# Six modulation units' column products moved from before the first expert pair to behind the last scatter, rank products placed directly behind the routing mask

## The reference

```python
mod = jax.nn.silu(c) @ w_ada[layer] + b_ada[layer]          # 6 x 1024 values
sh1, sc1, g1, sh2, sc2, g2 = jnp.split(mod[:, None, :], 6, axis=-1)
...
hcur = rms_norm(x, norm2_g[layer]) * (1 + sc2) + sh2
x = x + g2 * hierarchical_moe(hcur, ...)                    # top-1 group of 4, top-2 experts in it
```

## Time and profile before

| what | us |
|---|---|
| three runs: median, lowest, highest | 1336.81, 1328.77, 1337.17 |
| profiled execution | 1328.29 |
| its span | 1326.6 |
| TensorE busy (share of the span) | 1217.2 (92%) |
| VectorE, ScalarE, GpSimd busy | 358.3, 291.9, 79.5 |

### The profile page before, as it was taken

One profiled execution on the slowest core, in us unless ns is written; L12 is line 12 of the kernel. 1 busy time (PEld: TensorE's weight loads), 2 busy tenths in 40 slices (PEclk: granted clock), 3 DMA queues, 4 the chain that ended last, 5 costly groups with the idle time before them and its releaser, 6 DMA issues.

```text
span 1326.6 us, 17378 instructions
## 1 busy us (share of the span) xinstructions
PE 1217.2 (92%) x7164; PEld 716.8 (54%) x7167; DVE 358.3 (27%) x1005; ACT 291.9 (22%) x584; POOL 79.5 (6%) x135
## 2 busy tenths in 40 slices
PE   4799999999999969977989999996799999999996
PEld 1566544634344348554354444342686877767772
DVE  0202514312111124851341122211140342342212
ACT  2212423100100121134211111001201455452101
POOL 2000011000000004000000000000000233200000
PEclk8899999899999989977979999999899999999998
DMA  9994999899999995520579999999434344334000
GB/s 337 316 382 168 309 334 368 349 426 428 429 428 428 421 330 159 176 78 0 223 301 401 425 430 428 429 427 396 165 127 149 121 147 147 113 106 139 0 16 32
DMA packets 89682, 351.18 MB, mean 265 GB/s; under 512 B 5108, under 2 KB 7324, under 8 KB 77340
## 3 DMA queue, kind: packets, MB, share of 16 engines
q1 hardware_dynamic: 83144, 340.94, 66.4%
q0 software_dynamic: 4960, 6.53, 2.3%
q10 hardware_dynamic: 1524, 2.95, 0.6%
HBM read 349.27 MB, written 1.13 MB: 264 GB/s over the span
## 4 chain that ended last, share of the span: by engine, by line
PE 79%; DMA 10%; ACT 4%; DVE 3%; issue 1%; SPq 1%; DVEq 0%; ACTq 0%
PE bank L423 26%; PE bank L703 20%; PE bank L435 12%; DMA ring<-in_moe_w_up 8%; PE bank L675 3%; PE bank L724 3%; DMA ring<-in_ev_w_in 2%; PE bank L458 2%; PE bank L471 2%; PE bank L933 1%; ACT arena L1001 1%; SPq L340 1%; PE bank L554 1%; PE bank L591 1%; PE bank L480 1%
## 5 line engine op out<-in xcount | busy, mean ns | idle before, releaser
L423 PE MATMUL bank<-arena,ring 128*128 128x256 f32 x1600 | 352.7, 382 | 7.4 <-DVE arena L1385 2.8
L703 PE MATMUL bank<-ring,arena 128*32 128x512 f32 x3072 | 336.3, 595 | 8.9 <-issue 4.5
L423 PEld LDWEIGHTS bank<-arena,ring 128*128 128x128 f32 x1600 | 303.3, 191 | 55.5 <-issue 8.3
L703 PEld LDWEIGHTS bank<-ring,arena 128*32 128x32 f32 x3072 | 101.6, 110 | 230.9 <-issue 228.2
L435 PE MATMUL bank<-ring,arena 128*128 128x512 f32 x352 | 157.7, 608 | 2.4 <-issue 2.4
L435 PEld LDWEIGHTS bank<-ring,arena 128*128 128x128 f32 x352 | 68.0, 195 | 88.9 <-issue 88.0
L458 PE MATMUL bank<-ring,c_rep 128*32 128x512 f32 x480 | 62.6, 655 | 12.5 <-DMA ring<-in_w_ada 8.3
L675 PEld LDWEIGHTS bank<-arena 128*128 128x128 f32 x512 | 62.6, 203 | 11.7 <-issue 11.7
L675 PE MATMUL bank<-arena 128*128 128x128 f32 x512 | 65.5, 290 | 0.0
L1753 DVE TENSOR_TENSOR arena<-arena,bank 128x512 f32<-128x512 f32 x16 | 11.0, 687 | 198.0 <-PE bank L703 198.0
L1048 ACT ACTIVATE arena<-bank 128x512 f32<-128x512 f32 x41 | 23.6, 594 | 169.4 <-PE bank L423 128.9
(11 more groups left out here) (280 smaller groups left out, 925.2 us busy)
## 6 DMA issues: line engine op xcount, KB each, us to landing
ring<-in_moe_w_gate SPq DMA_DIRECT2D x32, 2048.0 KB, 14.3
ring<-in_moe_w_up SPq DMA_DIRECT2D x32, 2048.0 KB, 17.2
ring<-in_moe_w_down SPq DMA_DIRECT2D x32, 2048.0 KB, 13.3
ring<-in_w_ada SPq DMA_DIRECT2D x24, 2048.0 KB, 15.5
ring<-in_w_in SPq DMA_DIRECT2D x16, 2048.0 KB, 9.5
ring<-in_w_c SPq DMA_DIRECT2D x6, 2048.0 KB, 8.1
ring<-in_ev_w_in SPq DMA_DIRECT2D x5, 2048.0 KB, 20.7
ring<-in_od_w_in SPq DMA_DIRECT2D x5, 2048.0 KB, 18.8
```

The source lines that it names most:

```text
L423: mm = pe.matmul(ps[k0][:, t * S:(t + 1) * S], w[:, k, c:c + P], rhs[:, k, :], start=(k == 0), stop=(k == KT - 1))
L703: mm = pe.matmul(bank[col:col + CHUNK, :], lhs[:, k, col:col + CHUNK], ring[:, s0 + e, cut], start=start, stop=stop, tile_position=(0, col))
```

## The change

Once per layer, in `experts(layer)` and what follows it:

```diff
@@ TensorE, experts(layer)
                 gate_row(gate, 1)
-                for n in range(units - 3):
+                for n in range(units - 4):
                     ada_main()
-                pe.wait_ge(sem("ada_part_taken"), units_before + 4)
-                ada_columns()
 
                 pe.wait_ge(sem("mask_ready"), layer + 1)
@@
                 pe.matmul(ps[4][:, 416:432], ones, mask[:, 1, :], start=False, stop=True)\
                   .then_inc(sem("rank_full"), 1)
-                for n in range(units - 1):
-                    ada_columns()
+                ada_main()
+                pe.wait_ge(sem("ada_part_taken"), units_before + 4)
                 pe.wait_ge(sem("over_ready"), layer + 1)
@@
                 pe.reg_load(split_reg, split[0:1, layer, 0:1])
+                pe.wait_ge(sem("ada_part_taken"), units_before + units)
                 gather(0)
-                pe.wait_ge(sem("ada_ready"), units_before + units)
                 clear_sums()
@@
                 results(PAIRS - 1)
                 scatter(PAIRS - 1)
+                for n in range(units):
+                    ada_columns()
                 pe.wait_ge(sem("late_ready"), layer + 1)
@@ TensorE, overflow(layer)
                 with pe.If(some > 0):
+                    pe.wait_ge(sem("ada_ready"), sum(ROUTE_UNITS[layer]))
                     pe.wait_ge(sem("x_summed"), layer + 1)
@@ VectorE, experts(layer)
                 left_over(layer)
-                route_cols(layer)
                 tokens_taken(0)
@@
                 ins.then_inc(sem("x_summed"), 1)
+                route_cols(layer)
                 return some
@@ GpSimd, overflow(layer)
                 with pool.If(some > 0):
+                    pool.wait_ge(sem("ada_cols_full"), sum(ROUTE_UNITS[layer]))
                     late_experts(layer)
```

## The result

The changed kernel takes 1335.64 us (median of 20 runs, 1330.39 to 1342.77), the kernel before 1331.01 (20 runs, 1323.44 to 1337.22): ratio 1.0035, 95% interval [1.0019, 1.0051]. It is slower by some 4.6 us, where I had forecast 1.5 faster.

A forecast was written before the change was run, and what follows sets the result against it. TensorE was taken to bound the kernel, then the weight stream's restart. Head gains 3.7 + 5.1 = 8.8 less the tail's 7.3 gave 1.5 faster: 1326.8 against the profiled execution, median 1335.3, range 1325 to 1341, chance 0.62.

The forecast's parts named there:

- Head of layer 0: Mask to first gather and pair 1's weights in layer 0: gather 4.8 earlier, weight-stream hole closed, gain 3.7.
- the 3.75 which I had called all that can be had: Layer 0's hole in the weight stream, 4.1 long: 3.75 of lost stream, claimed as the most that could be gained.
- up to 0.9: New wait before gather(0): a moved main at half clock, 3.6 for 1.8, would cost up to 0.9; taken as 0.
- TensorE's wait ahead of the gather: After the moved main and overflow count, TensorE was to wait 1.2 for DVE's picks before the gather.
- Head of layer 1: Mask to pair 1's weights in layer 1: gather 3.8 earlier and 1.3 shorter, all fitting the hole, gain 5.1.
- the 3.88 of 'issue' staying as it is: The stop behind layer 1's gather, before the first pair, was to keep its 3.88.
- the low end of 3.8: Smallest gain forecast for layer 1's head, whose range was 3.8 to 6.4 around 5.1.
- the middle, 1.3: Layer 1's gather, 6.37 long: full clock gives 2.6 more, half clock nothing; 1.3 was taken.
- The tail: Last scatter to squares, waiting for 48 column records and route_cols: cost 3.2 + 4.1 = 7.3; 5.8 at full clock.
- A: Rival: columns behind the scatter run at 1.2 GHz; from length 6.9 cost outweighs 8.8; 1340.2 to 1344.0; chance 0.18.
- B: Rival: weights bound the stage anyway, so the head gains nothing and the tail costs 7.3; 1344.1; chance 0.08.
- C: Rival: layer 1's 3.88 stop goes, with full-clock gathers and tails; 8.2 gained, 1328.6; sign no "issue" there; chance 0.12.

The follow-up runs named there:

- e6: Changed kernel with route_cols moved behind the next norm's work on DVE and 95 instructions of long-met waits at TensorE's start: 1323.54 us, ratio 0.9939 to the kernel before.
- e1: Changed kernel with 96 long-met waits (48 instructions) added at TensorE's start, nothing else: 1337.65 us, ratio 1.0035 to the kernel before.
- e2: Changed kernel with route_cols moved on DVE from ahead of x_ready to behind the next norm's work, TensorE's order unchanged: 1327.42 us, ratio 0.9976 to the kernel before.
- e5: Changed kernel with 190 long-met waits (95 instructions) at TensorE's start, so layer 1's pairs lie in their code blocks as before: 1331.5 us, ratio 1.0012.
- e11: The kernel of e6 run once more, unchanged: 1323.03 us, ratio 0.9937 to the kernel before.
- e3: Changed kernel with both e1's 48-instruction shift and e2's later route_cols: 1328.31 us, ratio 0.9971 to the kernel before.
- e7: The kernel before with e1's 96 waits (48 instructions) at TensorE's start and nothing else: 1332.55 us, ratio 1.001.

## Why the prediction was wrong

*The number.* The median of 1335.64 lies 0.3 from the forecast 1335.3 by luck. I had built that on a median of 1336.8 for the kernel before, from three runs; over 20 it is 1331.01, and the change lost 4.6 where I had it win 1.5.

*Head of layer 0: right.* The gather was due 4.8 earlier and came 4.6 earlier; the hole closed; 3.7 forecast, 4.3 measured. That is 0.6 more than the 3.75 which I had called all that can be had, and e6 has 4.6; where the rest comes from was not looked into. With the main at half clock the gather is 1.2 to 1.5 later (e1, e2), where I had allowed up to 0.9 and taken 0. TensorE's wait ahead of the gather was given as 1.2 and is 1.4, behind the picks, as named.

*Head of layer 1: wrong, by 4.4.* Of 5.1 there came 0.7. The step that failed is "the 3.88 of 'issue' staying as it is". I had seen that it was a branch's stop and weighed the rule for it, but not that the removal of 95 instructions ahead of the branch changes where a second fetch falls. With the code back in its place (e5) pair 1's weights are issued 3.7 earlier, just under the low end of 3.8; at the end of the last scatter it is 2.9 in e5, 3.8 in e6 and 3.3 in e11. What is still short of 5.1 is the gather, which mostly kept the half clock (5.79 for 6.37, 0.6 where I had taken the middle, 1.3), and a stop of 4.43 for 3.88. The longer stop has a plain account: the instruction packet starts 8.10 behind the gather's start in e5 and 8.13 in the kernel before, and the stop ends 3.0 later in both. So in these two traces what the gather wins in length goes into the stop itself.

*The tail: mechanism right, size wrong, by 2.4.* The step is "I take 3.2 + 4.1"; it measured 5.0 + 4.7. The waits and their order were as described (e2 takes the whole price away: squares at 2.96 and 3.33, 8 us in all), the columns are 7.4 and 7.1 long. I had let the clock fall 5.2 and 3.9 behind the scatter, as it fell when TensorE was idle. It fell at 2.8 and 3.1. In e5's layer 1 it held, and the 48 records took 5.26, as the full clock gives, and in e1's layer 0 5.27; so the price differs from one execution to the next, 2.9 in these two and 5.2 in e5's layer 0. By the Trainium skill's rule on the gate (TensorE: Matmul & The Clock Gate, Part 1: The HAM clock gate) alone, the two layers together cost 5.8; the trace is against it, since PE reads busy 1.00 of 1.00 at 0.50.

*The rivals.* A came nearest: its point, columns longer than 6.9, was passed (7.4 and 7.1), and 9.7 outweighs even the forecast 8.8. By its sum that alone is a loss of 0.9; the other 3.8 came from the heads (5.0 for 8.8). B is not what happened: layer 0's stream gained, and in e6 both layers' gains reach the end. C was wrong in the sign: the wait without a name did change because TensorE's code moved, and it grew.

*Open.* With some 235 instructions left in its block the path's next fetch starts 1.6 to 3.5 later behind the beginning of `down` than with 188 or 140; what in the code sets off a fetch isn't settled, and the profile names no reason for "issue". Nor is it known how much of e5's 1.0012 over e6's 0.9939 changes with the clock of the columns.

## What to carry to other kernels

Work moved "behind" a producer is only off the path if no in-order queue holds it ahead of the signal others wait for: here one small VectorE instruction ahead of `x_ready` cost 9.7 over two layers, and behind it nothing. Removing instructions ahead of rarely taken paths moves the code of those paths, and where the profile shows "issue" at a branch, shift the code by some waits that are met at once and look again before judging the edit: it was worth 3 to 5 here by the medians (e5 beside the changed kernel, e6 beside e2; the intervals overlap, the traces agree), and other shifts nothing (e1, e3, e7). Look for the instruction queue's packets beside such a stop, and at when they start: here a stop ended 2.9 to 3.1 behind the start of one, so its length tells how late the fetch began, not how long it took.

## What the runs showed of the hardware that I had not expected

Matmuls of one column hold TensorE at full busy share and still lose the clock: 48 of them took 5.26 with it held and 7.1 to 8.1 with it lost behind the scatter, 10.33 at 0.50 throughout. And stops at a branch of 1.08, 3.57, 4.13 and 4.43 us, with the weight stream at 5, 305, 428 and 427 GB/s, all end 2.9 to 3.1 behind the start of a packet of instructions that takes 1.0 to 1.1 in each: the stops differ by when the packet starts, from 1.8 ahead of the stop to 1.4 into it.
